# Opening of a hybrid decoder step: first conditioning slabs of 256 channels, eight half-depth chunks, parked sums

## The reference, cut to what matters

```
mod = silu(c) @ w_ada + b_ada                   # c: 1 prompt row and 8 sample rows; w_ada 2048 x 12288
shift1, scale1, gate1, shift2, scale2, gate2 = split(mod, 6)
h = rmsnorm(x, norm1_g) * (1 + scale1) + shift1
q, k, v, qb, kb, vb, r, glr = split(h @ w_in)   # w_in 2048 x 6160
x = x + gate1 * (concat(attention(q, k, v), gla(qb, kb, vb, glr) * silu(r)) @ w_out)
h2 = rmsnorm(x, norm2_g) * (1 + scale2) + shift2
y = x + gate2 * ((silu(causal_conv(h2 @ w_up_gate)) * (h2 @ w_up_u)) @ w_down)
```

## Time and profile before

| | |
|---|---|
| median of 3 runs | 1542.83 us (1542.47 to 1544.98) |
| profiled execution | span 1544.0 us (no other time is given for it) |
| PE (matmul) busy | 1514.8 us, 98% |
| PE weight load busy | 1372.8 us, 89% |
| VectorE, ScalarE, GpSimd busy | 875.7, 633.9, 52.4 us |
| moved by DMA | 370.98 MB, 240 GB/s on average |
| DMA busy share | 0.9 or more in the first 100 us |

### The profile page before, as it was taken

One profiled execution on the slowest core, in us unless ns is written; L12 is line 12 of the kernel. 1 busy time (PEld: TensorE's weight loads), 2 busy tenths in 40 slices (PEclk: granted clock), 3 DMA queues, 4 the chain that ended last, 5 costly groups with the idle time before them and its releaser, 6 DMA issues.

```text
span 1544.0 us, 27862 instructions
## 1 busy us (share of the span) xinstructions
PE 1514.8 (98%) x11762; PEld 1372.8 (89%) x11762; DVE 875.7 (57%) x1509; ACT 633.9 (41%) x873; POOL 52.4 (3%) x89
## 2 busy tenths in 40 slices
PE   8999999999999889999999999999999999999999
PEld 4877888888888557768899999999999999999999
DVE  3655676666667435557454555555554565656574
ACT  3433444434445215235333333334333445545453
POOL 2000000001111000000000000000000000000000
PEclk8999999999999999999999999999999999999999
DMA  9998777777777997997644444454545444454541
GB/s 354 400 355 346 307 257 257 257 259 267 255 288 270 413 414 309 422 363 292 251 164 164 164 164 169 159 184 147 188 146 182 163 172 178 166 181 172 178 176 53
DMA packets 62283, 370.98 MB, mean 240 GB/s; under 512 B 7431, under 2 KB 7913, under 8 KB 27081
## 3 DMA queue, kind: packets, MB, share of 16 engines
q1 hardware_dynamic: 56096, 351.08, 60.6%
q0 software_dynamic: 5904, 17.93, 3.4%
q10 hardware_dynamic: 162, 0.22, 0.0%
HBM read 359.32 MB, written 9.88 MB: 239 GB/s over the span
## 4 chain that ended last, share of the span: by engine, by line
PE 89%; DMA 5%; DVE 3%; SPq 2%; ACT 1%; issue 1%; POOL 0%; ACTq 0%; DVEq 0%
PE ps L989 26%; PE ps L990 25%; PE ps L991 25%; PE ps L941 4%; PE ps L934 1%; SPq L710 1%; DMA ring<-in_w_ada_early 1%; DMA ring<-in_w_out 1%; DMA ring<-in_cache_k_win 1%; DMA proj<-in_tables 1%; ACT whi L1501 1%; DVE wlo L2028 1%; PE ps L1321 1%; DMA ring<-in_w_ada 1%; PE ps L1290 1%
## 5 line engine op out<-in xcount | busy, mean ns | idle before, releaser
L989 PE MATMUL ps<-hhi,whi 128*128 128x288 f32 x3136 | 934.0, 298 | 3.1 <-DVE wlo L1871 1.6
L990 PE MATMUL ps<-hlo,whi 128*128 128x288 f32 x3136 | 922.6, 294 | 0.0
L991 PE MATMUL ps<-hhi,wlo 128*128 128x288 f32 x3136 | 922.5, 294 | 0.0
L989 PEld LDWEIGHTS ps<-hhi,whi 128*128 128x128 f32 x3136 | 589.0, 188 | 38.8 <-issue 29.9
L990 PEld LDWEIGHTS ps<-hlo,whi 128*128 128x128 f32 x3136 | 589.2, 188 | 0.7
L991 PEld LDWEIGHTS ps<-hhi,wlo 128*128 128x128 f32 x3136 | 588.9, 188 | 0.0
L1492 ACT ACTIVATE whi<-ring 128x1024 fp32r<-128x1024 f32 x178 | 185.7, 1060 | 200.7 <-PE ps L991 200.7
L1864 DVE TENSOR_TENSOR wlo<-ring,whi 128x1024 fp32r<-128x1024 f32 x178 | 212.0, 1221 | 78.8 <-ACT whi L1492 78.4
L2028 DVE TENSOR_TENSOR wlo<-ring,whi 128x1024 fp32r<-128x1024 f32 x96 | 117.0, 1223 | 79.6 <-ACT whi L1501 79.5
L1501 ACT ACTIVATE whi<-ring 128x1024 fp32r<-128x1024 f32 x96 | 100.8, 1053 | 130.1 <-PE ps L991 114.2
L2545 DVE TENSOR_TENSOR wlo<-ring,whi 128x1024 fp32r<-128x1024 f32 (+1 forms) x94 | 105.7, 1132 | 56.2 <-ACT whi L1805 56.2
(11 more groups left out here) (298 smaller groups left out, 905.4 us busy)
## 6 DMA issues: line engine op xcount, KB each, us to landing
ring<-in_w_up SPq DMA_DIRECT2D x88, 1024.0 KB, 4.8
ring<-in_w_down SPq DMA_DIRECT2D x32, 1408.0 KB, 6.1
ring<-in_w_ada SPq DMA_DIRECT2D x42, 1024.0 KB, 6.8
ring<-in_w_in SPq DMA_DIRECT2D x28, 1024.0 KB, 6.5
ring<-in_w_ada_early SPq DMA_DIRECT2D x22, 1024.0 KB, 7.5
proj<-in_w_ada SPq DMA_DIRECT2D x22, 1024.0 KB, 11.0
ring<-in_w_in_early SPq DMA_DIRECT2D x20, 1024.0 KB, 9.3
ring<-in_w_out SPq DMA_DIRECT2D x16, 1024.0 KB, 13.2
```

What stands on the lines that cost most here:

```text
L989: mm(out, w_hi, x_hi, start=start, stop=False)
L990: mm(out, w_hi, x_lo, start=False, stop=False)
L991: return mm(out, w_lo, x_hi, start=False, stop=stop)
```

## The change

The columns of slabs 0 to 7 of w_ada are ordered anew: slabs 0 to 3 now hold shift and scale of channel tiles 0 and 1 (256 channels each), slabs 4 to 7 those of tiles 2 and 3. The first eight chunks become half-depth chunks: 2 contraction tiles × 512 columns (four output tiles, a "pair of units"), same bytes and same number of matmuls. `HALVES` gives their order: contraction tiles 0, 1 for pairs 0, 1, 2, 3; then tiles 2, 3 for pairs 3, 0, 1, 2. Pair 3 stays in its banks from chunk 3 to chunk 4; the sums of chunks 0, 1 and 2 are copied to proj ("parked") and chunks 5, 6 and 7 are added to them on VectorE. A chunk now uses four banks and has four copies or additions, not two.

```diff
+PAIR_TILES = (28, 32, 36, 24)
+HALVES = ((0, 0), (0, 1), (0, 2), (0, 3), (1, 3), (1, 0), (1, 1), (1, 2))
+LEAD_HOMES = "SSLLRRSSLLSSRRLLSSLLSSLL"
-        ADA_AT = [s // 2 * 2 + 1 for s in range(22)] + [22, 22]
+        ADA_AT = [4 + s // 2 for s in range(8)] + [s // 2 * 2 + 1 for s in range(8, 22)] + [22, 22]
 # SP
-            for s in range(8):
+            for s in range(3):
                 ada_load(s)
             in_load(0)
+            for s in range(3, 6):
+                ada_load(s)
             in_load(1)
-            for s in range(2):
-                sp.wait_ge(raw_used, s + 3)
-                ada_load(s + 8)
+            for s in range(6, 8):
+                ada_load(s)
+            sp.wait_ge(raw_used, 3)
+            ada_load(8)
+            in_load(2)
+            sp.wait_ge(raw_used, 4)
+            ada_load(9)
             ada_load(10)
             sp.wait_ge(*NT[0].upto("roots"))
             sp.wait_ge(*NM[0].upto("diag"))
             ada_load(11)
+            lead_load(4)
+            lead_load(5)
-            asks = [(2 * w - 5.3, in_load, w) for w in range(2, 48)]
-            asks += [(ADA_AT[a_ - 4] + 1.2, lead_load, a_) for a_ in range(4, 24)]
+            asks = [(2 * w - 5.3, in_load, w) for w in range(3, 48)]
+            asks += [(ADA_AT[a_ - 6] + 1.2, lead_load, a_) for a_ in (6, 7)]
+            asks += [(ADA_AT[a_ - 4] + 1.2, lead_load, a_) for a_ in range(8, 24)]
 # POOL, before the bias tables
-            pool.wait_ge(full[1], 16)
+            pool.wait_ge(*PT_.upto("x15"))
+            pool.wait_ge(*NA[0].upto("q5"))
 # PE
             vectors()
+            early_slab(0)
             for k in range(8, KD):
                 x_turns(k)
-            for s in range(4):
-                early_slab(s)
-            norm_roots()
+                if k == 11:
+                    early_slab(1)
+                if k == 13:
+                    norm_roots()
+            early_slab(2)
+            idle_products(6, 2)
+            early_slab(3)
+            idle_products(6, 1)
+            early_turn(0, 0)
             idle_products(6, 4)
-            early_slab(4)
-            biases()
-            early_turn(0, 0)
-            for s in range(5, 8):
-                early_slab(s)
-            idle_products(3, 1)
-            early_turn(0, 1)
-            idle_products(7, 8)
+            def half_chunk(j):
+                z = HALVES[j][0]
+                pe.wait_ge(lo_done, CH_IN + j + 1)
+                for r in range(4):
+                    if j in (1, 2, 3):
+                        pe.wait_ge(part_v if r % 2 else part_a, 2 * (j - 1) + r // 2 + 1)
+                    elif j > 4:
+                        pe.wait_ge(tile_v if r % 2 else tile_a, 2 * (j - 5) + r // 2 + 1)
+                    for k in range(2):
+                        if j in (0, 4):
+                            pe.wait_ge(*NL[0].upto(f"l{2 * z + k}", 0))
+                        ...
+                last.then_inc(used, 1)
+                if j == 0:
+                    early_slab(4)
+                if j == 1:
+                    early_slab(5)
+                    early_slab(6)
+                    biases()
+                    early_slab(7)
+                if j == 2:
+                    early_turn(0, 1)
 # ScalarE
+            in_hi(0)
             ada_rows(0, 0)
+            norm_hi(0, (0, 1))
+            in_hi(1)
+            half_copy(0, 0)
+            half_copy(0, 2)
+            in_hi(2)
+            in_hi(3)
+            half_copy(1, 0)
+            half_copy(1, 2)
             ada_rows(0, 1)
+            half_copy(2, 0)
+            in_hi(4)
+            half_copy(2, 2)
+            norm_hi(0, (2, 3))
+            in_hi(5)
+            in_hi(6)
+            in_hi(7)
+            half_copy(4, 0)
+            half_copy(4, 2)
 # VectorE, after the x copies (the sums, diagonals and roots of the norm now stand between these)
+            norm_rooted(0)
+            in_lo(0)
+            half_mod(0)
+            half_norm(0)
+            in_lo(1)
             rel_copies()
+            half_copy(0, 1)
+            half_copy(0, 3)
+            in_lo(2)
+            in_lo(3)
+            half_copy(1, 1)
+            half_copy(1, 3)
+            norm_rooted(1)
+            biases()
+            norm_rooted(2)
+            half_copy(2, 1)
+            in_lo(4)
+            half_copy(2, 3)
+            half_mod(1)
+            half_norm(1)
+            in_lo(5)
+            in_lo(6)
+            norm_rooted(3)
+            in_lo(7)
+            half_copy(4, 1)
+            half_copy(4, 3)
```

More of the change, by code:

```diff
@@ L131, in weight_slabs @@
 def weight_slabs(w_in, w_out, w_up, w_down, w_ada):
+    early = np.arange(2 * D).reshape(2, KD // 4, 2, 256)
+    early[:, 0] = early[:, 0].transpose(1, 0, 2).copy()
+    first = column_blocks(w_in[0, 0:D, 2048:5120], 4, 512)[:, 0].reshape(6, P, 4, 512)
+    first = np.stack([first[PAIR_TILES[q] // 4 - 4][:, 2 * z:2 * z + 2] for z, q in HALVES])
+    first = first.reshape(4, 2, P, 1024).transpose(0, 2, 1, 3).reshape(4, P, 2048)
     down = w_down[0].reshape(4, 11, P, D // 256, 256).transpose(3, 0, 2, 1, 4)
@@ L136, in weight_slabs @@
             "w_down": np.ascontiguousarray(down.reshape(D // 256, 4, P, 11 * 256)),
-            "w_ada_early": column_blocks(w_ada[0, :, 0:2 * D], 4, 512)}
+            "w_in_first": np.ascontiguousarray(first),
+            "w_ada_early": column_blocks(w_ada[0][:, early.reshape(-1)], 4, 512)}
 def key_units(cache):
@@ L435, in build @@
         w_down = a["w_down"]
[L437 removed]
+        first_rows = [rows_hi_lo[:, c:c + 2048].rearrange("p (k c) -> p k c", k=4) for c in (640, 2688, 5760, 7808)]
         def slab(s, k, c):
@@ L2040, in _, with half_copy @@
                     v.tensor_copy(small[:, :], ps[:, 4, 0:313]).then_inc(*PV_.step("vectors"))
-            rel_copies()
-            norm_roots()
-            biases()
-            norm_rooted(0)
-            dve.wait_ge(*AT.upto("turn_b", 0))
-            mod(0)
-            norm_group(0)
-            norm_tiles(0, 0)
-            for j in range(1, 4):
-                in_lo(j)
-            for j in range(1, 4):
-                norm_rooted(j)
+                if k == 9:
+                    norm_sums()
+                if k == 11:
+                    norm_diagonals()
+                if k == 13:
+                    norm_roots()
+            norm_rooted(0)
[3 more added lines that the diff above has]
+            in_lo(1)
+            rel_copies()
+            def half_copy(j, r):
+                if r < 3:
+                    dve.wait_ge(tile_done, 3 * j + r + 1)
+                else:
+                    dve.wait_ge(used, CH_IN + BUFS + j + 1)
+                tile, out = proj[:, half_tile(j, r), :], ps[:, half_banks(r), 0:TOK]
+                if j <= 4:
+                    v.tensor_copy(tile, out).then_inc(tile_v if j == 4 else part_v, 1)
+                else:
+                    dve.wait_ge(part_v if r % 2 else part_a, 2 * (j - 5) + r // 2 + 1)
+                    v.tensor_tensor(tile, out, tile, ALU.add).then_inc(tile_v if r % 2 else tile_a, 1)
+            half_copy(0, 1)
[5 more added lines that the diff above has]
+            norm_rooted(1)
+            biases()
+            norm_rooted(2)
[10 more added lines that the diff above has]
+            half_copy(4, 3)
             def early_copy(j):
@@ L2257, in queries @@
                 last.then_inc(*SQ.step("qd"))
-            for j in range(1, LAST + 1):
-                if j <= SPLIT:
+            for j in range(HALVED - 3, LAST + 1):
+                if HALVED - 3 < j <= HALVED:
+                    for r in range(4):
+                        half_copy(j - 1, r)
+                elif HALVED < j <= SPLIT:
                     early_copy(j - 1)
```

136 lines of the change are left out of this document (103 added, 33 removed).

## The result

The changed kernel takes 1550.61 us (median of 5 runs, 1548.51 to 1553.09); the kernel before, run beside it, 1544.7 us (5 runs, 1542.47 to 1545.9). The medians are 5.9 us apart. The ratio on record is 1.0046, with a 95% interval of 1.0035 to 1.0057 (it isn't the quotient of the two medians, which is 1.0038): slower. The forecast was 1546.5 with a range of 1540.5 to 1550.0: the direction and the place are right, the size is too small, and the time lies 0.6 us above the range.

The account below looks back on a forecast made before the run. DMA loads and PE were both taken as full in the opening. Chunk 8 3.7 us late plus 0.2 for the clock, less 0.2 for the deeper queue, gave 3.7 on 1542.8: 1546.5 us, range 1540.5 to 1550.

Parts of the forecast that it names:

- The landing: w3, the w_in slab of chunks 6 and 7, is 18th in SP's queue and lands at 62.8 us (61.3 to 65).
- The wait and its shape: Chunk 5 waits for chunk 4's copies behind splits wanting w3: PE idles 4.8 us before quarter 0, 1.9 before quarter 1.
- The clock behind the wait: PE's clock may fall after idling ahead of chunk 5, costing 0 to 1.5 us; 0.2 was put.
- The rest up to chunk 8: After chunk 5, slabs 10 to 15, chunks 6 and 7 and one turn take 12.95 us; chunk 8 starts at 83.45.
- Chunk 0: The first product's chunk starts at 35.0 us, 9 us earlier than before, with three idle products added at 0.25 us each.
- The base: The shift of 3.7 us is added to the kernel before's median of 1542.8 us.
- Its own range: The forecast's range from the ends of the landing (-1.5, +2.2): 1544.5 to 1549 us; chance 0.60.
- (a): At chunk 5's start, w3 is not the gate and PE alone decides: up to 3.0 us faster, 1539.8; chance 0.15.
- (b): The shift is swallowed later, in a stage that waits for loads alone: 1542.8 us; chance 0.12.
- (c): Opening worse: half clock through chunk 0 and again behind the wait (1.5 us), w2 gap of 1 us: 1549; chance 0.10.
- (d): Loads run at 374 GB/s from the fourth slab on, 4.5 us later: 1551 us; chance 0.03.

Follow-up runs that it names:

- a1: Changed kernel with chunk 4's four copies moved ahead of the splits of chunks 6 and 7 on ScalarE and VectorE; 1548.0 us, ratio 1.0032.
- a2: Changed kernel with w_in slab 3 asked for ahead of slabs 12 and 13, engines' orders left alone; 1545.89 us, ratio 1.0015.
- b1: a3 plus two idle products ahead of the vectors' turns in the opening; 1548.72 us, ratio 1.0034 to the kernel before.
- a4: Changed kernel with idle products in its pause: 14 ahead of chunk 5, 3 between its first and second quarter; 1553.3 us, ratio 1.0068.
- a6: Changed kernel with 20 idle products in the opening, orders as changed; 1554.42 us, ratio 1.0072 to the kernel before.
- a5: a3 with 20 idle products in the opening; 1550.23 us, ratio 1.0044 to the kernel before.
- b2: a3 run once more, the same program; 1546.1 us, ratio 1.0016 to the kernel before.
- c1: a3 with VectorE's additions of chunks 5, 6, 7 ahead of the splits of chunks 8, 9, 10; 1545.18 us, ratio 1.0004.
- d2: c1 with one idle product after each of the first eight turns of x; 1542.88 us, ratio 0.9993 to the kernel before.
- b3: Kernel before with two idle products ahead of the vectors' turns; 1545.49 us, ratio 1.0013 to the kernel before.
- a3: Changed kernel with the edits of a1 and a2 together; 1546.42 us, ratio 1.0024 to the kernel before.
- c3: c1 with SP's order as in the changed kernel (w_in slab 3 behind slabs 12 and 13); 1547.36 us, ratio 1.0023.
- c2: c1 with two idle products ahead of the vectors' turns; 1544.68 us, ratio 1.0007 to the kernel before.
- d1: c1 with five idle products: after turns 1, 3, 5, 7 of x and ahead of the vectors' turns; 1543.1 us, ratio 0.9997.
- a8: a3 with 30 idle products in the opening; 1552.57 us, ratio 1.0065 to the kernel before.
- d3: Kernel before with the five idle products of d1; 1546.47 us, ratio 1.0016 to the kernel before.
- a7: Kernel before with 20 idle products in the opening; 1548.58 us, ratio 1.0041 to the kernel before.

## Why the prediction was right in direction and short in size

**The landing (62.8 predicted).** w3 is issued at 43.20 and takes 19.8 us: 63.0. Counting 1 MB slabs in SP's queue from the trace of before held within 0.2 us. The place in the queue decides here, not the moment of the issue: a1 issues w3 at 47.66 and it lands at 62.98; asked for two slabs earlier, it lands at 59.0 in a2 and at 58.2 in b1.

**The wait and its shape.** Quarter 0 at 65.45 (65.3), quarter 1 at 68.15 (68.0), PE ready at 58.8 (60.5), so PE idled 6.6 us and not the 4.8 of the sum. b1, with the changed kernel's opening, has no wait ahead of chunk 5; a1 and a2 each take the cause away in another place; a4 shows the two copies as what releases PE; a6 against a5 prices it with the openings alike. This step is shown.

**The clock behind the wait (0.2 predicted).** This is the step that failed, the mis-sized term. The prediction put quarter 0's slow run under the second quarter's wait, bounded the rest by 0 to 1.5 from the earlier trace rows, and took 0.2 with no row for so small a share. The half clock lasted until 71.6 us, and the three quarters took 4.16 us, not 2.5. Measured: 1.6 us, by a4, a little above the bound. The profiles at hand have the longer stretch behind the longer wait: 10.2 us behind 6.6 of idle PE here, 6.8 behind 5.3 in b1, 3.4 behind 3.7 in b2 (and 6.8 behind a6's 2.9 and 1.7).

**The rest up to chunk 8 (12.95).** 85.38 - 72.31 = 13.07. Sum of the steps: chunk 8 was predicted 3.9 late with the 0.2 and came 5.6 late; 1.4 of the 1.7 is the clock, 0.2 the landing, 0.1 the rest.

**Chunk 0 (35.0).** 33.57. Two errors nearly cancel in it: an idle product costs 0.5 us (1.99 us for 4), not the 0.25 that was counted, and the half clock was 3.4 us instead of the 10.2 that had been carried over unchanged from the trace of before. Neither moved quarter 0, since PE came 6.6 us too early for the landing; whether the longer wait lengthened the half clock behind it isn't shown. The prediction also speaks of pauses in the half-clock stretch of the earlier trace rows, where PE reads 10.20 busy of 10.20 us; the last section has the pause that stands ahead of it.

**The base.** The forecast added the shift to the median of 3 runs, 1542.8. With 5 runs that median is 1544.7, and over the later comparisons of 20 to 29 runs each it is 1543.1 to 1543.6. The forecast with the measured clock term and the base of its own comparison would be 1546.5 + 1.4 + 1.9 = 1549.8; 0.8 us of the result stays unassigned. The prediction's "1.2 above the median" sets a span (1544.0) against times of runs. Where both are listed a time is 1.5 to 1.6 us above its span, so that execution took about 1545.6 us by estimate, 2.8 above the median; the forecast itself doesn't use this. Its own range should start at 1546.5 - 1.5 = 1545.0, not at 1544.5.

**The rivals.** (a), PE alone decides, was wrong for the changed kernel, but its mechanism appears once both waits are mended: c1 has chunk 8 at 75.86, where PE alone was to give 76.75. That c1's profiled execution took 1539.74 us, close to its 1539.8, is luck in part, since 2.0 us of it come from behind 500 us. (b) is refuted: the distance is 5.6 at chunk 8, at 151 and at 503 us and still 5.7 at 686 us. (c) had half of it: the half clock behind the wait for 1.5 us, but no slow opening in the profile. The 5 runs, 1548.5 to 1553.1, may hold it; that isn't shown. (d) asked for 374 GB/s throughout, and the landing at 63.0 excludes it. The Trainium skill ("DMA: Bandwidth & Descriptors", Specifications) gives about 358 GB/s as the limit; the window from 17.0 to 20.4 us shows 420.

**What stays open.** What decides between a long and a short stretch at half clock in the opening, in one and the same program. Why d2, 2.0 us earlier at chunk 8 and 2.5 us shorter in the profiled span than the kernel before, is only 0.6 us faster in the median. Its later stretches at half clock (6.8 us at 518.3, 3.4 at 682.2) are no answer: the profile of the kernel before has 10.2 us of them too (3.4 each at 522, 577 and 686). The runs beside d2 point elsewhere. The profiled execution of the kernel before was a long one (about 1545.6 us by the estimate above, against a median of 1543.46), and its two runs with d2's mean clock of 0.996 took 1542.48 and 1542.75 us, no longer than d2's median of 1542.88. By these two runs d2 gains by its steady clock and not by its orders, whose gain the fill spends; two runs don't show it. And the price of the early w3 once the engines' orders are mended, in a trace with a good opening.

## What to carry to other kernels

When an order is rewritten, list for each instruction that frees a bank what stands ahead of it on its own engine, and when the inputs of that land: a copy of 0.4 us behind a split that wants a slab cost a wait of 6.6 us here, and moving the copy forward uncovered the next of its kind, and that one's mend a third. A gain ahead of the first product is worth only what loads and the granted clock leave of it: in b3 PE came 2.5 us earlier to a load that landed at the same time. Compare profiles at one named instruction well behind the change, and look at the clock of the stretch between before explaining the rest. Where a kernel's runs spread, sort them by their mean clock before looking at the median.

## What was not expected of the hardware

The half-clock stretch of the opening, over turns of 128 × 128 tiles on which PE reads busy for 16.65 of 17.1 us, lasted 3.4 us in b1's execution, 10.2 in b2's and 17.1 in a3's, the last two of one program. Between a3 and b2 it moved chunk 0 by 3.4 us (38.92 and 35.56). Just ahead of it, or as it begins, most profiles have a short wait of PE for a small vector (`a_out_g`), which ends at 15.9 to 16.6 us. It is 1.2 us in a1 and a3, 0.9 in c3 and 0.8 in a2 (17.1 us at half clock each), 1.0 in b2 and 0.7 in the kernel before (10.2), 0.2 in c1 (6.8), 0.8 in the changed kernel and 0.6 in a4 (3.4). b1, c2 and d1, with idle products in that place, have no such wait and 3.4 us; a5 to a8 and d2, filled further, have neither the wait nor the low clock. So the pause goes with the fall but doesn't fix the length: 0.8 us stands ahead of 3.4 and of 17.1. The Trainium skill ("TensorE: Matmul & The Clock Gate", Part 1) ties the half rate to an idle PE; the wait of 6.6 us followed by 0.50 agrees, while b1, c2 and d1 fell to half with no wait over 0.2 us in the 4 us ahead.

Two idle products put in this pause made the kernel before 2.4 us slower in the median. They took the half clock away at 16.9 us, PE came earlier to the bias products, waited 2.5 us there for the tables, and the half clock came at 33.6 us instead, over real work (chunk 0 at 48.65, not 44.23). d3 repeats this (2.0 us, 33.1 us, 49.10), a7, whose longer fill lets PE come at 37.56 us, has neither. One idle product among the turns costs 0.46 us: eight take 3.70 us.
